# Differential attention of a two-block transformer kernel: score halves in turn into two sets of three banks, one pass of weights by a ratio of sums, norms with tokens on partitions

## What is computed

```python
q = rmsnorm(dq.reshape(..., DIFF_HEADS, 2, 64), q_norm_g)      # axial rope on q and k of x
s = einsum('bhqcd,bhkcd->bhcqk', q, k_all) * 64 ** -0.5
p = softmax(s, axis=-1)
a = p[:, :, 0] - lam * p[:, :, 1]
od = einsum('bhqk,bhkd->bhqd', a, v_all)
mix = concat([rmsnorm(og, gla_norm_g) * silu(r),
              rmsnorm(od, diff_norm_g) * (1 - lam_init)]) @ w_out
x = x + gt1 * mix
```

## Time and profile before

| | us |
|---|---|
| median of 3 runs | 1610.55 (1609.94 to 1611.12) |
| span of the profiled execution (first to last instruction) | 1612.3 |
| own time of the profiled execution | not listed apart from the span |
| PE busy | 1565.7 (97%) |
| DVE busy | 931.3 (58%) |
| ACT busy | 734.0 (46%) |
| POOL busy | 125.4 (8%) |
| mean granted TensorE clock | 0.992 |

### The profile page before, as it was taken

One profiled execution on the slowest core, in us unless ns is written; L12 is line 12 of the kernel. 1 busy time (PEld: TensorE's weight loads), 2 busy tenths in 40 slices (PEclk: granted clock), 3 DMA queues, 4 the chain that ended last, 5 costly groups with the idle time before them and its releaser, 6 DMA issues.

```text
span 1612.3 us, 19639 instructions
## 1 busy us (share of the span) xinstructions
PE 1565.7 (97%) x7839; PEld 1249.2 (77%) x7839; DVE 931.3 (58%) x1409; ACT 734.0 (46%) x1159; POOL 125.4 (8%) x89
## 2 busy tenths in 40 slices
PE   8999999899999999999999899999989999999998
PEld 2677876677788888888878677788778888888887
DVE  4666777876744433334545555365757786257745
ACT  4444446765333222223443666545556453234432
POOL 0000213640000000000010011130010000000000
PEclk9999999899999999999999999999999999999999
DMA  9541111104334232322232122143213232333221
GB/s 383 198 159 41 52 54 53 65 1 146 130 133 140 75 110 103 105 77 90 96 105 65 67 72 72 40 144 99 85 34 105 79 117 73 104 112 93 87 81 66
DMA packets 49262, 157.67 MB, mean 98 GB/s; under 512 B 5618, under 2 KB 12402, under 8 KB 48660
## 3 DMA queue, kind: packets, MB, share of 16 engines
q1 hardware_dynamic: 47632, 151.74, 28.5%
q10 hardware_dynamic: 1540, 4.69, 0.8%
HBM read 154.31 MB, written 2.10 MB: 97 GB/s over the span
## 4 chain that ended last, share of the span: by engine, by line
PE 79%; DVE 10%; ACT 7%; issue 2%; DMA 1%; POOL 0%; SPq 0%; DVEq 0%; ACTq 0%
PE pall L2291 18%; PE pall L2293 17%; PE pall L2292 17%; PE pall L2823 2%; PE pall L2825 2%; PE pall L2824 2%; PE pall L2325 1%; PE pall L2327 1%; PE pall L2326 1%; DVE wlo L1335 1%; PE pall L2366 1%; ACT whi L591 1%; DMA mod<-in_weights 1%; ACT e L892 1%; DVE statd L1682 1%
## 5 line engine op out<-in xcount | busy, mean ns | idle before, releaser
L1335 DVE TENSOR_TENSOR wlo<-raw,whi 128x1024 fp32r<-128x1024 f32 (+2 forms) x261 | 290.6, 1114 | 298.9 <-ACT whi L591 298.6
L591 ACT ACTIVATE whi<-raw 128x1024 fp32r<-128x1024 f32 (+2 forms) x263 | 247.0, 941 | 182.6 <-PE pall L2293 164.9
L2291 PE MATMUL pall<-h5h,whi 128*128 128x512 f32 x320 | 124.9, 390 | 1.0 <-DVE wlo L1335 1.0
L2293 PE MATMUL pall<-h5h,wlo 128*128 128x512 f32 x320 | 124.5, 389 | 0.0
L2292 PE MATMUL pall<-h5l,whi 128*128 128x512 f32 x320 | 124.5, 389 | 0.0
L2291 PE MATMUL pall<-h2h,whi 128*128 128x512 f32 x320 | 124.5, 389 | 0.0
L2292 PE MATMUL pall<-h2l,whi 128*128 128x512 f32 x320 | 124.5, 389 | 0.0
L2293 PE MATMUL pall<-h2h,wlo 128*128 128x512 f32 x320 | 124.5, 389 | 0.0
L2291 PEld LDWEIGHTS pall<-h5h,whi 128*128 128x128 f32 x320 | 60.1, 188 | 13.9 <-DVE wlo L1335 1.4
L2293 PEld LDWEIGHTS pall<-h5h,wlo 128*128 128x128 f32 x320 | 60.1, 188 | 12.6
L2292 PEld LDWEIGHTS pall<-h2l,whi 128*128 128x128 f32 x320 | 60.1, 188 | 12.6
(11 more groups left out here) (506 smaller groups left out, 3714.1 us busy)
## 6 DMA issues: line engine op xcount, KB each, us to landing
raw<-in_weights SPq DMA_DIRECT2D x204, 512.0 KB, 3.5
mraw<-in_wmod SPq DMA_DIRECT2D x32, 512.0 KB, 4.8
mod<-in_weights SPq DMA_DIRECT2D x16, 512.0 KB, 15.4
raw<-in_weights SPq DMA_DIRECT2D x25, 256.0 KB, 2.6
raw<-in_weights SPq DMA_DIRECT2D x32, 192.0 KB, 2.3
xT<-in_x SPq DMA_DIRECT2D x1, 2048.0 KB, 13.5
xT<-in_x ACTq DMA_DIRECT2D x1, 2048.0 KB, 7.9
out_y<-xT SPq DMA_DIRECT2D x5, 256.0 KB, 2.3
```

Source lines behind the costliest of these rows:

```text
L591: e.activation(whi[j % 3][:, 0:cols(j)], raw[j % 4][:, 0:cols(j)], ACT.Copy).then_inc(s.hi, 1)
L1335: e.tensor_tensor(wlo[j % 3][:, 0:n], raw[j % 4][:, 0:n], f(whi[j % 3][:, 0:n]), ALU.subtract).then_inc(s.lo_v, 1)
L2291: e.matmul(o_, a[:, kk, :], xh(k), start=(k == 0), stop=False)
L2293: mm = e.matmul(o_, b[:, kk, :], xh(k), start=False, stop=(k == nk - 1))
```

## The change

1. Scores. The two halves of a unit fill three banks (1536 columns, `score_cols`); even units take banks 3 to 5, odd ones 0 to 2. The middle bank holds columns of both halves. The twelve matmuls alternate between half 1 (array rows 64 to 127) and half 0 (rows 0 to 63); in the middle bank half 0 starts when half 1 has ended there (a wait on `s.sc`). Row maxima of both halves wait for the whole unit.
2. Weights. One pass on DVE: `e0 + e1 * (-lam * s0 / s1)`, i.e. without the division by `s0`. POOL no longer scales. The factor `s0` is left in the output and taken care of in the norm: the epsilon is multiplied by `s0` squared (`es`, one 128x1 product per unit on POOL).
3. Turned weights go through bank 6 in two parts (four transposes and two), with the value product of the unit before between them; the value products of all heads go to bank 7. TensorE makes the scores of unit n+1 ahead of unit n-2's transposes.
4. Norms `h` (GLA heads 2 and 3), `dq3` and `d0` to `d3`: the sum is taken with the squares as stationary operand and one or two columns of ones moving (`token_sums`), so that tokens lie on partitions and 4 or 8 columns hold all sums; root and Newton step run on 128x4 or 128x8 (`token_root`, `token_add`, `token_newton`), and four transposes of a broadcast column bring the result back to 128x512 in bank 6 (`spread`). Squares of heads 0 to 2 are made on POOL, their copy out of PSUM on DVE. ACT copies and squares GLA heads 2 and 3 ahead of the root of `dq2` (`out_copies`).
5. Low parts of keys and queries from head 1 on, and of mixed heads 4 to 6, move from DVE to POOL (semaphore `dp` counts POOL's work in a fixed order).
6. `w_out`: the first halves of wo0 to wo2 are made inside the loop at n = 15 to 17; their second halves are cut into k = 4 to 5, k = 6 and k = 7. Banks for wo come from `wo_bank`.
7. The constants `64 ** -0.5` and `1 - lam_init` are multiplied into the gains once at the start, by two DVE operations on 128x1.

```diff
+        def score_cols(n):
+
+            b = 0 if n % 2 else 3
+            return pall[:, 512 * b:512 * b + 1536].rearrange("p (c k) -> p c k", c=2)
...
+        wo_bank = (3, 4, 5, 0, 1, 2, 3, 4)
...
+            def out_copies():
+                for h in (2, 3):
+                    w.wait_ge(s.hop, h + 1)
+                    e.activation(HN[h], bank(4 + h % 2), ACT.Copy).then_inc(s.lq, 1)
+                w.wait_ge(s.p_sum, job["h1"])
+                for h in (2, 3):
+                    w.wait_ge(s.lq, h - 1)
+                    e.activation(hq[h - 2][:, 0:512], HN[h], ACT.Square).then_inc(s.hosq, 1)
...
-            out_square(3)
-            out_root(2)
-            out_root(3)
...
+            def turned(i, part):
+
+                a, b = (0, 4) if part == 0 else (4, 6)
+                w.wait_ge(s.tp, 2 * i + part + 1)
+                w.wait_ge(s.pv, i - 2)
+                e.activation(PT[i % 3][:, a:b, :], win(bank(6, 128 * (b - a))), ACT.Copy).then_inc(s.ta, 1)
...
+            w.wait_ge(s.dev, 4)
+            e.activation(tmp[3][:, :], tmp[2][:, :], ACT.Square).then_inc(s.dsq, 1)
+            token_root("d3", 4, 128)
+            diff_high(3)
...
-            out_norm(2)
-            out_norm(3)
...
+                w.wait_ge(s.ex, 2 * n + 2)
+                w.wait_ge(s.dcw, 2 * n + 1)
+                w.wait_ge(s.lam_v, 4)
+                e.tensor_scalar(sd[:, col + 3:col + 4], sd[:, col + 7:col + 8], sd[:, col + 2:col + 3], nlam, ALU.mult,
+                                ALU.mult).then_inc(s.dcw, 1)
+                w.wait_ge(s.dcw, 2 * n + 2)
+                e.scalar_tensor_tensor(e0[:, :], e1[:, :], sd[:, col + 3:col + 4], e0[:, :], ALU.mult,
+                                       ALU.add).then_inc(s.dw, 1)
...
-                e1 = EB[n % 3][1][:, :]
-                w.wait_ge(s.drec, 2 * n + 1)
-                e.tensor_scalar(e1, e1, sd[:, col + 3:col + 4], nlam, ALU.mult, ALU.mult).then_inc(s.dnl, 1)
...
+                product(1, 1, qh, kh)
+                product(0, 0, qh, kh)
+                product(1, 1, qh, kl)
+                product(1, 1, ql, kh).then_inc(s.sc, 1)
+                product(0, 0, qh, kl)
+                product(1, 0, qh, kh)
+                product(0, 0, ql, kh)
+                product(1, 0, qh, kl)
+                w.wait_ge(s.sc, 3 * n + 1)
+                product(0, 1, qh, kh)
+                product(0, 1, qh, kl)
+                product(1, 0, ql, kh).then_inc(s.sc, 1)
+                product(0, 1, ql, kh).then_inc(s.sc, 1)
...
+                if n < 15:
+                    diff_scores(n + 1)
+                else:
+                    mix_out(n - 15, 0, 4)
...
+                if n >= 2:
+                    turn(n - 2, 0)
+                if n >= 3:
+                    diff_products(n - 3)
+                if n >= 2:
+                    turn(n - 2, 1)
+            diff_products(15)
+            for m in range(2):
+                mix_out(m, 4, 6)
+            diff_sums(3)
+            mix_out(2, 4, 6)
+            mix_out(0, 6, 7)
+            spread("d3", 6, 1, 0, (s.dft, 4))
...
-            mix_out(1, 0)
-            mix_out(2, 0)
+            for m in range(1, 3):
+                mix_out(m, 6, 7)
             for m in range(3):
-                mix_out(m, 4)
+                mix_out(m, 7, 8)
```

More of the change, by code:

```diff
@@ L266, in win, with rbuf @@
             return a.rearrange("p (w t) -> p w t", t=128)
+        def rbuf(k):
+            return R[(k + (k > job["dq2"])) % 2]
         eps = small[:, 0:1]
@@ L931, in _ @@
-            root("d3", bank(7), 512, 128)
-            w.wait_ge(s.dft, 4)
-            e.activation(mixh[:, 7, :], tmp[0][:, :], ACT.Copy, scale=1.0 - LAM_INIT).then_inc(s.dfh, 1)
-            w.wait_ge(s.kql, 8)
+                if n in (10, 14, 17):
+                    diff_high((10, 14, 17).index(n))
+                if 12 <= n < 15:
+                    hi(J[("wo", n - 12, 0)])
+                if n >= 2:
+                    turned(n - 2, 1)
+            e.dma_start(cbx2[:, :], ap["cc"][:, 0, :].to_broadcast([128, 1024])).then_inc(s.cc, 16)
@@ L1351, in inv @@
                 w.wait_ge(s.rstd, job[name])
[L1352 removed]
+                return rbuf(job[name])[:, 0:n]
             def add_square(g, k):
@@ L2615, in last_query, with token_sums, spread @@
                     mm.then_inc(s.used, 1)
-                    freed[b] = [(s.lq, 1)]
+                    freed[b] = [(s.lq, 3)]
+            def token_sums(name, b, squares, mat, groups):
+                fill(b)
+                n = 0
+                for src in squares:
+                    for k in range(4):
+                        mm = e.matmul(bank(b, groups, n), src[:, 128 * k:128 * k + 128], mat[:, 0:128:128 // groups], start=True,
+                                      stop=True)
+                        n += groups
+                mm.then_inc(s.p_sum, 1)
+                freed[b] = [(s.rsum, job[name])]
+            def spread(name, b, groups, c, user):
+                fill(b)
+                w.wait_ge(s.rstd, job[name])
+                for k in range(4):
+                    to = bank(b, 128, 128 * k)
+                    if groups == 1:
+                        t = e.transpose(to, tr[:, c + k:c + k + 1].to_broadcast([128, 128]), ident[:, :])
+                    for g in range(groups if groups > 1 else 0):
+                        r = tr[:, c + 2 * k + g:c + 2 * k + g + 1].to_broadcast([128, 64])
+                        t = e.matmul(to[64 * g:64 * g + 64, :], r, ident[:, :], start=True, stop=True)
+                t.then_inc(s.tspr, 1)
+                freed[b] = [user]
             last_query(0)
@@ new lines, in diff_scores, with product @@
+            def diff_scores(n):
+                i, h, qt = diff_units[n]
+                b = 0 if n % 2 else 3
+                qs = slice(128 * qt, 128 * qt + 128)
+                for k in range(b, b + 3):
+                    fill(k)
+                w.wait_ge(*((s.dp, dp["q", h]) if h else (s.dfl, 2)))
+                qh, ql, kh, kl = Qh[h % 2], Ql[h % 2], Kh[h % 2], Kl[h % 2]
+                def product(c, shared, q_, k_):
+                    p = slice(64 * c, 64 * c + 64)
+                    keys = slice(*((0, 512), (512, 768), (256, 768), (0, 256))[2 * c + shared])
+                    return e.matmul(score_cols(n)[:, c, keys], q_[p, qs], k_[p, keys], start=(q_ is qh and k_ is kh),
+                                    stop=(q_ is ql))
+                product(1, 1, qh, kh)
[11 more added lines that the diff above has]
+                product(0, 1, ql, kh).then_inc(s.sc, 1)
+                for k in range(b, b + 3):
+                    freed[k] = [(s.mx, 2 * n + 2), (s.ex, 2 * n + 2)]
@@ new lines, in turn, with diff_products @@
+            def turn(i, part):
+                a, b = (0, 4) if part == 0 else (4, 6)
+                fill(6)
+                w.wait_ge(s.dw, i + 1)
+                for k in range(a, b):
+                    c = slice(128 * k, 128 * k + 128)
+                    t = e.transpose(bank(6, 128, 128 * (k - a)), EB[i % 3][0][:, c], ident[:, :])
+                t.then_inc(s.tp, 1)
+                freed[6] = [(s.ta, 2 * i + part + 1)]
+            def diff_products(i):
+                _, h, qt = diff_units[i]
+                qs = slice(128 * qt, 128 * qt + 128)
+                if qt == 0:
+                    fill(7)
+                w.wait_ge(s.ta, 2 * i + 2)
+                w.wait_ge(s.vg, 6 + 6)
+                for k in range(6):
+                    mm = e.matmul(bank(7)[:, qs], Vd[:, k, 128 * h:128 * h + 128], PT[i % 3][:, k, :], start=(k == 0),
+                                  stop=(k == 5))
+                mm.then_inc(s.pv, 1)
+                freed[7] = [(s.dev, h + 1)]
```

440 lines of the change are left out of this document (228 added, 212 removed).

## The result

The changed kernel takes 1616.08 us in the median of 11 runs (1614.74 to 1621.12), the kernel before, in the same comparison, 1612.95 (1609.94 to 1613.89): ratio 1.0028, 95% interval 1.002 to 1.0037. That is slower, by 3.1 us in the medians and 4.5 by the ratio; forecast were 3 us less. The profiled execution is the one at the median: 1616.08, span 1614.2 (the span is some 1.8 us shorter than the time). The profiled execution of the kernel before, span 1612.3, must by the same token have taken about 1614.1, which is above every run of it counted here: its trace shows more waiting or half clock than its median does.

The account below looks back on a forecast made before the run. TensorE, at 4.35 us a unit, was taken to bound the loop. wo3 starting 4.7 us earlier, less 1.7 for half clock, made 3.0 us less: 1610.55 - 3.0 = 1607.5 us, range 1600 to 1615.5.

Parts of the forecast that it names:

- TensorE at 4.35 is the engine that sets the pace: Attention loop of the kernel before: TensorE's 4.35 us a unit bounds it, with DVE close behind where a norm falls in.
- DVE's last unit 354.8: Loop sum: first maxima, fifteen units of 3.3 us, norms, bank 6, clock and coupling; DVE begins the last unit at 354.8.
- 1.0 for the half clock at the start: Start of the attention loop: half clock on TensorE adds 1.0 us to the loop's sum.
- 0.5 us at each of six places: Bank 6 in the loop: TensorE waits for ACT or DVE to empty it, 3 us together, 0 to 1.0 each.
- POOL has no wide operation left in the chain: Loop, weights: POOL's 128x1 product per unit put at nothing; if late, the exponential four units on would wait.
- 1.0 us ahead of DVE, at 353.8: Start of the loop's tail: TensorE about 1.0 us ahead of DVE, at 353.8, when DVE begins the last unit.
- the tail itself: TensorE's work from 353.8 to the last value product: 19.8 us, ending at 373.6 against 375.66 before.
- the seam: Last value product to wo3: 14.5 us instead of 17.1, with TensorE idle 1.05 and 3.7 us.
- Twelve score matmuls: Scores of one unit on TensorE: side by side they take 1.05 us, about half of 2.1.
- A: Rival, whole stretch: bank 6, coupling and clock cost nothing; gain 9.9 us, time 1600.6; chance 0.23.
- C: Rival, scores: halves not side by side in the middle bank, or alternation costs a drain; 1610 to 1616; chance 0.07.
- B: Rival, loop: TensorE held at half clock, 6.6 us a unit, so the loop runs at its pace; 1615.0; chance 0.2.

Follow-up runs that it names:

- the first experiment: Kernel before, with only the scores of the two halves issued in turn, each into its own pair of banks: 1611.44 us, ratio 1.0003.
- d2: Changed kernel with the last query's nine products put ahead of the GLA heads' sum, into TensorE's idle time: 1612.92 us.
- c3: Changed kernel with DVE's order alone changed, operations that empty banks 6 or 7 ahead of reciprocal and weights or rotation: 1613.71 us, ratio 1.0011.
- f1: Changed kernel with POOL's order alone changed, wide operations moved away from DVE's tiny steps of the last query's norm: 1616.09 us.
- a1: Kernel before, with only the scores of the two halves issued in turn (same run as the first experiment): 1611.44 us, ratio 1.0003.
- the rest alone: Changed kernel with its scores issued one half after the other again, all else as changed: 1620.57 us, ratio 1.0056.
- d3: Changed kernel with w_out matmuls back behind the loop, Silu and wo3's parts earlier, DVE's order, query products and unit 1's scores moved: 1606.69 us, ratio 0.9966.
- a2: Changed kernel with the scores of unit 1 issued right behind the GLA heads' sum, ahead of the last query's products: 1616.13 us.
- b1: Changed kernel with its scores one half after the other again (same run as the rest alone): 1620.57 us, ratio 1.0056.
- c1: Changed kernel with every low part that POOL computes in this stretch computed twice, 13 more operations: 1620.62 us.
- a4: Changed kernel with the Silu and its table loads earlier on ACT, and wo3's high and low parts made earlier: 1611.75 us.
- a3: Changed kernel with 24 matmuls of w_out, first halves of wo1 and wo2, issued behind the loop again: 1612.52 us.
- d1: Changed kernel with 14 useless 128x512 matmuls in TensorE's idle time ahead of wo3: 1614.92 us, ratio 1.0017.

## Why the prediction was wrong

**Wrong: what bounds the loop.** "TensorE at 4.35 is the engine that sets the pace" was not enough. A ring over three engines and three pairs of banks, 4.33 us, stands level with it as soon as TensorE's work is removed; the first experiment finds it. I had added up each engine's busy time per unit and never the way of one bank around. For the changed kernel itself this did little harm, because it has the banks for a second ring in flight: DVE's own 3.3 us a unit, as forecast, is seen from 351.13 to 354.38, behind which three tiny steps of a norm follow.

**Wrong: the loop's sum, the step that failed.** Forecast for DVE's last unit 354.8, measured 359.05. From first to last maxima it is 71.9 us instead of 66.1 (and 1.8 of those 66.1 I had counted twice, as first maxima and again in fifteen whole units), less 1.5 because the first came at 287.18 rather than 288.7. Where the terms were too small:

- "1.0 for the half clock at the start": the half clock came 5 us earlier than before, over the sum of the GLA heads (3.4 us for its 16 passes, 0.95 for eight where the clock is full) and the query products, so that the scores of unit 1 were late: DVE idle for 4.93 us. The fill of d2 alone gains 3.2.
- "0.5 us at each of six places" for bank 6, and nothing for bank 7. The small round trips are 0.47 to 0.69, as forecast, but where TensorE waits for a DVE operation that itself stands behind weights or a rotation, it is 2.04, 2.18 and 1.52. I named bank 6 as a place and never walked DVE's queue at that moment; that heads 0 to 3 now share bank 7 I left out altogether. The edit of DVE's order alone (c3) gains 2.4.
- "POOL has no wide operation left in the chain": right, but it has wide operations beside the chain. The mean of the weights is 1.22 us where one alone takes 1.02, which is 3.2 us over the loop, and two tiny steps took 1.2 each. How much of this is on the path stays open: the same stretch remained in f1. The Trainium skill has the rule, in SBUF — State Buffer, section "SBUF: two separate sides": a pair of ports is lent to either GpSimd or a DVE operation with two SBUF inputs for a whole instruction, and the other one blocks. The rows of POOL and DVE above agree: the DVE step begun at 313.53 ends with POOL's at 314.7. The maxima, which read PSUM, are never stretched (940 to 958 ns, all 32).

**Wrong: where TensorE is when the loop's tail begins.** I set it 1.0 us ahead of DVE, at 353.8. It was at 360.89, 1.8 behind DVE, since behind the last scores it still turns unit 12 and multiplies unit 11. That is 2.8 of the 6.7 us by which the last value product is late (380.3 instead of 373.6); the loop is 4.25 of it, and the tail itself was right (19.4 instead of 19.8).

**Right, or nearly: scores, sums and the seam.** Twelve score matmuls take 1.25 us from their first start to the next operation, where it was 2.13 (1.05 forecast); a sum takes 0.95 at full clock (0.96 forecast); from the last value product to wo3 it is 14.3 us (14.5 forecast), with idle times of 0.83 and 3.55 (1.05 and 3.7 forecast), the second ended by wo3's low part; and 3.4 us at half clock behind it cost the 1.7 I had set. The hole that the change made by moving work out of its cover is therefore the best supported part of the loss: closing it gains 3.6 or 4.3 by the medians, 2.7 or 3.4 by the ratios.

**Rivals.** A didn't come. C fell: the halves run side by side in a1 and in the changed kernel (1.25 us for twelve). B came in amount: 17.1 us at half clock in the loop, as many as in the trace of before, and its 1615.0 is near the result. But its mechanism is a part only: of the 6.1 us between the gain forecast (3.0) and the loss measured (3.1), 3.2 come back when the first stretch is put off (d2), 2.4 by DVE's order with as much half clock up to 430 us in its trace as in the changed kernel's, 20.5 us (c3). I gave a slower outcome 0.24, too little for a change that puts three engines level, two banks in everybody's hands, and cover where it isn't needed. I also took the span of the profiled execution, 1612.3, for its time: it was some 3.5 us above the median and not 1.75, and the rows that I summed carry this.

**Open.** The 9 us of "the rest alone" are not fully divided. Seam (about 4), DVE's order (2.4) and start (3.2) overlap with the clock, whose stretches move with every edit; how much the norms with tokens on partitions save or cost by themselves wasn't tried. All edits together (d3) give back more than the whole loss: 1606.69 is 4.7 us below the kernel before, where the forecast was 3.0 below.

## What to carry to other kernels

Before making one engine's step shorter, follow one buffer once around: writer, readers, writer again. If that ring is as long as the engine's busy time, the shorter step buys nothing without more buffers, and the buffers taken from others must be walked in the same way, with the reader's place in its own queue. And work moved out of a stretch into an earlier gap is not free if it was the cover of a chain: price the hole, and the clock behind it.

## What was not expected of the hardware

- The granted clock answers to idle time, but not to its length alone. Ahead of wo3 a hole of 3.54 or 3.55 us was followed by 3.4 us at 1.2 GHz in four kernels (the changed one, a2, b1, d2); in two (c3, f1) 6.8 us at 1.2 GHz began inside it; in c1 there was none. Holes of 1.19 (a4) and 1.97 (a3) were followed by none. In the loop a hole of 2.17 or 2.18 us at bank 7 was followed by half clock in a2, a4 and d2 and not in a3, d1 and the changed kernel. In the changed kernel the clock fell at 283.2, inside an idle time of 1.64 us that came 1.3 us behind another of 1.69, and stayed at half for 10.2 us although TensorE was busy without a break from 284.4 on.
- A matmul with one moving column costs nearly as much as one with 128: eight passes take 0.95 to 1.03 us at 2.4 GHz (0.80 to 0.97 from their start to the next operation's, 0.10 to 0.12 each, where the value products are 0.11 to 0.12 apart) and 1.84 at 1.2 GHz. Keeping only one column of the sum saved TensorE nothing; it saved DVE and ACT their operations over 128x512.
- A DVE operation of 128x4 elements took 1.80 us beside a wide POOL operation in c1 (0.15 alone), and the one beside it 1.67.
